# Two feed-forwards whose down products are formed by seven products a pair of chunks instead of eight

## The reference, cut to what matters

```python
# block 1, hidden width 2816 = 22 chunks of 128
g = h @ w_gate ; u = h @ w_up
x = x + (silu(g) * u) @ w_down
# block 2, hidden width 4096 = 32 chunks of 128
y = square(relu(h @ w_up_2)) @ w_down_2
x = x + rms_norm(y) * gain
```

## Time and profile before

| | us |
|---|---|
| median of 3 runs (758.26 to 759.86) | 758.54 |
| the profiled execution, its own time | 758.59 |
| its span, first to last instruction | 757.3 |
| TensorE busy | 739.8 |
| VectorE busy | 457.8 |
| ScalarE busy | 373.3 |
| GpSimd busy | 112.5 |
| transfers | 130.46 MB, mean 172 GB/s |

### The profile page before, as it was taken

The page is one execution under the profiler, slowest core; times in us unless marked ns, Lnnn a source line. Parts: engine busy times, 40 slices in busy tenths (PEclk is TensorE's granted clock), DMA queues, the critical chain, the costliest instruction groups (busy, mean ns, idle before and its releaser), DMA issues.

```text
span 757.3 us, 11043 instructions
## 1 busy us (share of the span) xinstructions
PE 739.8 (98%) x4394; PEld 641.1 (85%) x4394; DVE 457.8 (60%) x635; ACT 373.3 (49%) x535; POOL 112.5 (15%) x138
## 2 busy tenths in 40 slices
PE   6999999999999999999999999999999999999996
PEld 5877778999999999888888888888779899998895
DVE  5898695766555555465747555674948754455433
ACT  6666754644444434285443534664338644444431
POOL 2867550100000000001110000000302111001110
PEclk9999999999999999999999999999999999999999
DMA  9642142787665666446536543474535766656511
GB/s 318 207 132 82 58 160 92 229 284 220 189 212 172 195 216 208 133 142 219 169 110 195 194 139 112 123 250 147 178 107 198 260 192 187 206 184 191 180 46 56
DMA packets 70179, 130.46 MB, mean 172 GB/s; under 512 B 5312, under 2 KB 29072, under 8 KB 70128
## 3 DMA queue, kind: packets, MB, share of 16 engines
q1 hardware_dynamic: 68144, 125.00, 52.3%
q0 software_dynamic: 1552, 4.20, 1.7%
q10 hardware_dynamic: 432, 0.56, 0.2%
HBM read 128.62 MB, written 1.05 MB: 171 GB/s over the span
## 4 chain that ended last, share of the span: by engine, by line
PE 93%; DVE 3%; DMA 2%; issue 1%; ACT 1%; SPq 0%; DVEq 0%; ACTq 0%
PE psum L453 41%; PE psum L888 29%; PE psum L506 12%; PE psum L930 2%; DMA w_raw<-in_w_in 2%; PE psum L680 1%; PE psum L601 1%; PE psum L546 1%; PE psum L631 1%; PE psum L1058 1%; PE psum L582 1%; PE psum L652 1%; DVE b_ratio L2154 0%; PE psum L992 0%; PE psum L1020 0%
## 5 line engine op out<-in xcount | busy, mean ns | idle before, releaser
L1908 DVE TENSOR_TENSOR w_lo<-w_raw,w_hi 128x1024 fp32r<-128x1024 f32 x225 | 275.2, 1235 | 158.3 <-ACT w_hi L1284 157.7
L1284 ACT ACTIVATE w_hi<-w_raw 128x1024 fp32r<-128x1024 f32 x231 | 241.2, 1059 | 180.7 <-PE psum L888 78.6
L888 PE MATMUL psum<-h_hi,w_hi 128*128 128x256 f32 x608 | 170.3, 284 | 0.6 <-issue 0.6
L888 PE MATMUL psum<-h_hi,w_lo 128*128 128x256 f32 x608 | 169.5, 283 | 0.0
L888 PE MATMUL psum<-h_lo,w_hi 128*128 128x256 f32 x608 | 161.8, 281 | 0.0
L888 PEld LDWEIGHTS psum<-h_hi,w_hi 128*128 128x128 f32 x608 | 114.7, 189 | 1.7 <-issue 0.7
L888 PEld LDWEIGHTS psum<-h_hi,w_lo 128*128 128x128 f32 x608 | 114.4, 188 | 0.0
L888 PEld LDWEIGHTS psum<-h_lo,w_hi 128*128 128x128 f32 x608 | 111.1, 189 | 0.7
L453 PE MATMUL psum<-w_hi,h_hi 128*128 128x512 f32 (+1 forms) x240 | 94.5, 394 | 0.0
L453 PE MATMUL psum<-w_hi,h_lo 128*128 128x512 f32 (+1 forms) x240 | 93.0, 387 | 0.0
L453 PE MATMUL psum<-w_lo,h_hi 128*128 128x512 f32 (+1 forms) x240 | 92.9, 387 | 0.0
(11 more groups left out here) (303 smaller groups left out, 992.7 us busy)
## 6 DMA issues: line engine op xcount, KB each, us to landing
w_raw<-in_w_in SPq DMA_DIRECT2D x77, 512.0 KB, 4.5
w_raw<-in_w_down SPq DMA_DIRECT2D x54, 512.0 KB, 4.3
w_raw<-in_w_up SPq DMA_DIRECT2D x32, 512.0 KB, 4.4
w_raw<-in_w_gate SPq DMA_DIRECT2D x44, 256.0 KB, 2.9
w_raw<-in_w_up SPq DMA_DIRECT2D x44, 256.0 KB, 3.4
w_raw<-in_w_out SPq DMA_DIRECT2D x16, 512.0 KB, 4.0
w_raw<-in_w_branch_a SPq DMA_DIRECT2D x4, 512.0 KB, 4.6
w_raw<-in_w_branch_b SPq DMA_DIRECT2D x4, 512.0 KB, 4.6
```

The costliest lines, as they stand in the source:

```text
L888: mm = pe.matmul(outs, x[:, cols], y[:, kc, :], start=kc == 0 and n == 0, stop=kc == KC - 1 and n == (1 if i == 0 else 2))
L1284: act.activation(T.w_hi[:, k % SLOTS, :], T.w_raw[:, k % RAW_SLOTS, :], ACT.Copy).then_inc(S.w_rounded, 1)
L1908: dve.tensor_tensor(T.w_lo[:, k % SLOTS, :], T.w_raw[:, k % RAW_SLOTS, :], T.w_hi[:, k % SLOTS, :], ALU.subtract).then_inc(S.w_cut, 1)
```

## The change

The hidden width is taken in pairs of chunks. For one pair the down product is a product of a 2 by 2 block matrix (two token tiles by two chunks) with a 2 by 2 block matrix (two chunks by two halves of the width): eight products of blocks. The changed kernel forms them by seven products (the Strassen-Winograd form). The sums of blocks that the seven products need are formed per pair: four sums of hidden blocks on VectorE (`sum_hidden`, `sum_hidden_2`, `sum_hidden_3`; blocks of 128x128), and four sums of weight blocks (128x512). Two of these sums are made by a transfer that adds into its destination, issued by GpSimd (`add_pair`), onto two copies of one block that SyncE loads with a broadcast source (`load_pair`); the other two are made by VectorE (`sum_pair`, `sum_pair_rest`). All seven weight blocks and seven hidden blocks are then rounded and cut. The seven products of all pairs add up in seven PSUM banks, and the four results are formed from the banks once at the end of each block (`form`, `form_last`). The last pair of each feed-forward is done plainly in eight products (`down_quarters`).

Seven banks for products leave one bank for the up product, so ScalarE copies the up product out of it at once (`take_up`, `take_hidden`). The up weights are laid out so that a fill is one chunk of 128 columns over the whole depth of 1024 (block 1: one fill of gate and one of up a chunk), and they are taken out of the ring of eight slots: four slots for up fills, four reused by one of the two pair buffers. GpSimd no longer squares in block 2.

```diff
+def quarters(w):
+    v = w.reshape(w.shape[0] // (2 * P), 2, P, 2, WIDE)
+    order = ((0, 0), (1, 1), (1, 0), (0, 1))
+    return np.ascontiguousarray(np.stack([v[:, c, :, n, :] for c, n in order], axis=2))
...
+        for f in range(2 * PAIRS1):
+            self.first["up1", f] = len(self.fills)
+            for w in range(2):
+                self.fills.append([(lambda raw: raw, a["up1"][f, :, w, :])])
...
+        for f in range(2 * PAIRS2):
+            self.first["up2", f] = len(self.fills)
+            self.fills.append([(lambda raw: raw, a["up2"][f])])
+        self.pairs = [a["down1"][i] for i in range(PAIRS1)] + [a["down2"][i] for i in range(PAIRS2)]
...
+PRODUCT = {1: (1, 0, 2), 2: (3, 2, 0), 3: (7, 1, 1), 4: (2, 6, 6), 5: (5, 3, 5), 6: (6, 5, 3), 7: (4, 4, 4)}
+EARLY, LATE, LAST = (1, 2, 3), (7, 5, 6, 4), (1, 6, 7, 4, 5, 2, 3)
+NEEDS = {1: 1, 2: 1, 3: 1, 7: 2, 5: 2, 6: 3, 4: 3}
+QUARTER_BANKS = {1: ((0, 0, 7), (1, 0, 2), (0, 1, 3), (1, 1, 4)), 2: ((0, 0, 7), (0, 1, 2), (1, 0, 3), (1, 1, 4))}
...
+    def load_pair(q):
+        raw = pair_place(q)[1]
+        if q == 0:
+            sp.wait_ge(S.cut_done, CUT["h2"] + 4)
+        elif q == 1:
+            sp.wait_ge(S.x_squared, 4)
+        elif q == FIRST2:
+            sp.wait_ge(S.attended2, TILES * HEADS2)
+            sp.wait_ge(S.x_added, 12)
+        elif q == FIRST2 + 1:
+            sp.wait_ge(S.x_squared, 8)
+        else:
+            sp.wait_ge(S.pair_cut, pair_parts(q - 1))
+        n = 1 if q in (LAST1, LAST2) else 2
+        sp.dma_start(T.pair_t[:, raw, 0:n, :], W.pairs[q][:, 3:4, :].broadcast_to([P, n, WIDE])).then_inc(S.pair_landed[raw], 16)
+        sp.dma_start(T.pair_raw[raw], W.pairs[q][:, 0:3, :]).then_inc(S.pair_landed[raw], 16)
...
+        j1, j2 = k - W.first["up1", 0], k - W.first["up2", 0]
+        if j1 % 4 == 3 and 4 < j1 < 4 * PAIRS1:
+            load_pair((j1 - 7) // 4)
+        if j1 == 4 * PAIRS1 - 1:
+            load_pair(LAST1)
+        if j2 % 2 == 1 and j2 > 2:
+            load_pair(FIRST2 + (j2 - 3) // 2)
+    load_pair(LAST2)
...
+    def up_first(name, ready, rounded, spread, right=None):
+        k0 = W.first[name, 0]
+        for s, two in ((0, 0), (1, 0), (0, 1), (1, 1), (2, 0), (2, 1), (3, 0), (3, 1)):
+            ks = (k0 + 2 * two, k0 + 2 * two + 1)
+            if s == 0:
+                for k in ks:
                     pe.wait_ge(*W.cut(S, k))
-                    if c % 2 == 0:
-                        pe.wait_ge(S.hidden_cut, cut0 + (steps - 1) * cut_per + c // 2 + 1)
-                s = k % SLOTS
-                for n, (x, y) in enumerate(((T.hid_hi, T.w_hi), (T.hid_hi, T.w_lo), (T.hid_lo, T.w_hi))):
-                    mm = pe.matmul(bank[4 + 2 * t + h][:], x[last][:, c, t * P:(t + 1) * P], y[:, s, cols],
-                                   start=False, stop=c == chunks - 1 and n == 2)
-                if n_bank == 3:
-                    mm.then_inc(S.w_used, 1)
-            if n_bank < 3:
-                mm.then_inc(S.bank_done, 1)
-    feed_forward("up1", "down1", FFN1_STEPS, 2, CUT["h2"], lambda i: (S.hidden_done, i + 1), 0, 1, True, NORM["h2"],
-                 turn_x_right)
-    turn_pairs(T.x, (0, 1), (2, 3), [[(S.x_added, 9), (S.hidden_done, 11)], [(S.x_added, 10)]])
-    turn_pairs(T.x, (2, 3), (4, 6), [[(S.x_added, 11)], [(S.x_added, 12)]])
+            if spread and (s, two) == (3, 0):
+                spread_scale()
+            for c in range(2):
+                pe.wait_ge(*((S.norm_rounded, rounded + s + 1) if c == 0 else (S.cut_rounded, ready + s + 1)))
+                for k in ks:
+                    up_chunk(k, 2 * s + c, bank[4 + k - k0][:, 0:SEQ], (0, 2), 1)
+            pe.wait_ge(S.cut_done, ready + s + 1)
+            for c in range(2):
+                for k in ks:
+                    mm = up_chunk(k, 2 * s + c, bank[4 + k - k0][:, 0:SEQ], (1,), 1)
+                    if 2 * s + c == KC - 1:
+                        mm.then_inc(S.w_used, 1)
+            if (s, two) == (0, 0) and right is not None:
+                right()
...
+    def down(q, products, first=False, last=False):
+        buf, i = pair_place(q)
+        pe.wait_ge(S.hidden_cut, q + 1)
+        for n_product, p in enumerate(products):
+            x, y, b = PRODUCT[p]
+            pe.wait_ge(S.pair_cut, pair_parts(q) + NEEDS[p])
+            x_hi, x_lo = T.hid_hi[:, i, x - 1, :], T.hid_lo[:, i, x - 1, :]
+            y_hi, y_lo = T.pair_hi[buf][:, y, :], T.pair_lo[buf][:, y, :]
+            for n, (u, v) in enumerate(((x_hi, y_hi), (x_hi, y_lo), (x_lo, y_hi))):
+                mm = pe.matmul(bank[b][:], u, v, start=first and n == 0, stop=last and n == 2)
+            if last:
+                mm.then_inc(S.product_done, 1)
+        if products == LATE:
+            mm.then_inc(S.pair_used, 1)
+    def down_quarters(block):
+        q = (LAST1, LAST2)[block - 1]
+        buf, i = pair_place(q)
+        pe.wait_ge(S.hidden_cut, q + 1)
+        pe.wait_ge(S.pair_cut, pair_parts(q) + 2)
+        for t, half, b in QUARTER_BANKS[block]:
+            if b != 7:
+                pe.wait_ge(S.formed, 3 * (block - 1) + max(1, b - 2))
+            for c in range(2):
+                y = ((0, 3), (2, 1))[c][half]
+                x_hi, x_lo = T.hid_hi[:, i, 2 * c + t, :], T.hid_lo[:, i, 2 * c + t, :]
+                y_hi, y_lo = T.pair_hi[buf][:, y, :], T.pair_lo[buf][:, y, :]
+                for n, (u, v) in enumerate(((x_hi, y_hi), (x_hi, y_lo), (x_lo, y_hi))):
+                    mm = pe.matmul(bank[b][:], u, v, start=c == 0 and n == 0, stop=c == 1 and n == 2)
+            mm.then_inc(S.quarter_done, 1)
...
+    up_first("up1", CUT["h2"], NORM["h2"], True, turn_x_right)
+    up_two(W.first["up1", 2], 3)
+    pe.wait_ge(S.up_taken, 2)
+    up_two(W.first["up1", 3], 7)
+    for i in range(2, PAIRS1):
+        if i == 2:
+            pe.wait_ge(S.spread_copied, 1)
+        down(i - 2, EARLY, first=i == 2)
+        chunk_up1(2 * i)
+        if i == 2:
+            pe.wait_ge(S.up_taken, 3)
+        down(i - 2, LATE, first=i == 2)
+        chunk_up1(2 * i + 1)
+    down(LAST1 - 1, LAST, last=True)
+    pe.wait_ge(S.up_taken, 2 * PAIRS1)
+    down_quarters(1)
...
+    up_first("up2", CUT["h4"], NORM["h4"], False)
+    up_two(W.first["up2", 4], 3)
+    for i in range(2, PAIRS2):
+        if i > 2:
+            pe.wait_ge(S.up_taken, 2 * PAIRS1 + i)
+            up_two(W.first["up2", 2 * i], 7)
+        else:
+            pe.wait_ge(S.up_taken, 2 * PAIRS1 + 2)
+        down(FIRST2 + i - 2, EARLY, first=i == 2)
+        if i == 2:
+            pe.wait_ge(S.up_taken, 2 * PAIRS1 + 3)
+        down(FIRST2 + i - 2, LATE, first=i == 2)
+    down(LAST2 - 1, LAST, last=True)
+    pe.wait_ge(S.up_taken, 2 * PAIRS1 + PAIRS2)
+    down_quarters(2)
...
+    take_up(0)
+    take_up(1)
+    round_fill(f + 6)
+    silu(0)
+    round_fill(f + 7)
+    silu(1)
+    for i in range(1, PAIRS1):
+        round_pair(i - 1, 0)
+        take_up(2 * i)
+        round_fill(f + 4 * i + 4)
+        silu(2 * i)
+        round_fill(f + 4 * i + 5)
+        round_hidden(i - 1)
+        round_pair(i - 1, 1)
+        round_pair(i - 1, 2)
+        if i == LAST1:
+            round_quarters(LAST1, 0)
+            round_quarters(LAST1, 1)
+        take_up(2 * i + 1)
+        round_fill(f + 4 * i + 6)
+        silu(2 * i + 1)
+        round_fill(f + 4 * i + 7)
+    round_hidden(LAST1)
+    copy_first(1)
...
+    round_to(f + 8)
+    round_pair(FIRST2, 0)
+    take_hidden(0)
+    take_hidden(1)
+    square_hidden(0)
+    square_hidden(1)
+    for i in range(2, PAIRS2 + 1):
+        q = FIRST2 + i - 1
+        if i == 2:
+            round_pair(FIRST2, 1)
+            round_pair(FIRST2, 2)
+            round_hidden(FIRST2)
+        if i < PAIRS2:
+            for part in range(3):
+                round_pair(q, part)
+            take_hidden(i)
+            round_to(min(f + 2 * i + 6, len(W.fills)))
+            square_hidden(i)
+        else:
+            for part in range(2):
+                round_quarters(q, part)
+        round_hidden(q)
+    copy_first(2)
...
+    def sum_pair(q):
+        i = pair_place(q)[1]
+        dve.wait_ge(S.pair_cut, pair_parts(q) + 1)
+        dve.wait_ge(S.pair_added[i], pair_adds(q))
+        step(dve.tensor_tensor(T.pair_raw[i][:, 0, :], T.pair_t[:, i, 0, :], T.pair_raw[i][:, 1, :], ALU.add))
+    def sum_pair_rest(q):
+        i = pair_place(q)[1]
+        own()
+        dve.tensor_tensor(T.pair_raw[i][:, 2, :], T.pair_raw[i][:, 0, :], T.pair_raw[i][:, 2, :],
+                          ALU.add).then_inc(S.pair_summed, 1)
...
+    for i in range(1, PAIRS1):
+        sum_hidden(i - 1, 2 * i)
+        cut_pair(i - 1, 0)
+        sum_hidden_2(i - 1)
+        scale_gate(2 * i)
+        sum_hidden_3(i - 1)
+        cut_fill(f + 4 * i + 4)
+        sum_pair(i - 1)
+        times_up(2 * i)
+        sum_pair_rest(i - 1)
+        cut_fill(f + 4 * i + 5)
+        cut_hidden(i - 1)
+        cut_pair(i - 1, 1)
+        cut_pair(i - 1, 2)
```

(111 more changed lines are left out.)

448 lines of the change are left out of this document (247 added, 201 removed).

## The result

The changed kernel takes 783.5 us (median of 4 runs, 780.5 to 793.7), the kernel before 758.7 beside it: ratio 1.031, 95% interval 1.028 to 1.034. The run of 793.7 was in a slower state of the chip, and the ratio leaves it out; the other three have a median of 783.4. The forecast was 760.2, its range 751.5 to 771. It is 24.8 us slower, where 1.6 was forecast.

What follows compares the result with a forecast made beforehand. TensorE, busy 739.8 of 757.3 us, was taken as the bound. Of 17.5 us of matmuls saved, seams gave all back: block 1 gains 2.4, block 2 loses 4.0, span 758.9, time 760.2, range 751.5 to 771.

Steps and rivals of the forecast that it cites:

- The failed step: Block 2's rounds: the adding transfer, at most 3 us, begins as the fills end and is hidden.
- the 9.6 us: Block 2's rounds: loop of pair load, fills, cut and rounding takes 9.6 us, under the round of 10.6.
- 9.5 of 10.6: Block 2's rounds: with adds at half rate (2.9 us), transfers take 9.5 of 10.6 us, same result with less room.
- seam 4: Start of block 2's feed-forward: fill 7 lands late, at 583.8, first hidden cut ends 592.9; TensorE loses 5.2 us.
- Seam 5: Block 2's first pair: TensorE waits 3.3 us for ScalarE to empty bank 3; the pair ends at 601.1.
- tail behind it: End of block 2: VectorE's forming, scaling and additions after the last matmul grow from 3.2 to 8.7 us.
- about 17: Whole kernel: sign that TensorE's busy time falls by about 17 us.
- Seam 1: Start of block 1's feed-forward: the first down matmul starts at 156.0, as before (155.90).
- Step 3: End of block 1: from 303.8, last hidden cut after 6.2 us, block 2 starts 16.5 later, at 320.3.
- B: Rival: transfers bound block 2 if the add takes over 4 us of engine time; 763 to 773, middle 768; chance 0.19.
- C: Rival: the ScalarE and VectorE loop bounds block 2, 11.0 us instead of 9.85 without overlap; 765 us; chance 0.14.
- A: Rival: the seams are cheap, as their chains lie beside TensorE's work; 753.7 us; chance 0.27.

Runs made afterwards that it cites:

- experiment 5: Changed kernel with block 2's 15 adding transfers turned into plain copies to an idle buffer that nothing waits for; 770.6 us (ratio 1.014).
- experiment 1: Changed kernel with block 2's 15 adding transfers sent into an idle buffer, so nothing waits for them; 777.5 us (ratio 1.026).
- 3: Changed kernel with block 2's pair loads issued behind the next two up fills instead of ahead, adds kept; 784.5 us (ratio 1.034).
- Experiment 6: Changed kernel without block 2's adding transfers and with its pair loads issued behind the next two up fills; 765.7 us (ratio 1.008).
- 2: Changed kernel with block 2's adding transfers left out altogether; 767.7 us (ratio 1.012).

## Why the prediction was wrong

**The failed step** is the sentence on the adding transfer: "It then begins as the fills end, and hides." Its price was right. Over the whole changed kernel the queue's time is 0.117 x 782.1 - 0.017 x 757.3 = 78.6 us for 25 adds, 3.1 each, where "at most 3" was taken. The Trainium skill, "Collectives: The Full Stack", section "The bandwidth ceiling: the fold count and why AG ≠ RS ≠ AR", says of the add in a collective's ReduceScatter that it needs two source reads and so has half the rate of a copy; for this transfer experiment 5 agrees, 2.9 us against 1.6. Two things made of that price were wrong.

First, the add is a link of the pair's own loop, in series, and I had left it out of the 9.6 us (whose own terms, 7.8 + 9 - 7.0, make 9.8). Load 9.7, add 8.8, sums and cuts 4.5 and hand-offs make 23.7 us for two rounds. With the median landing of 5.5 for the add the same loop would take 20.4, an estimate, and fit into two rounds of 10.6. So it is not the add as such that breaks the loop, but the adds that go out beside the next pair's load: they begin as the fills end, as forecast, and don't hide. TensorE's two long waits and the one of 1.7 us ahead of 679.24 each follow on such an add, landed at 617.6, 744.2 and 675.8.

Second, I compared engine time with the round (9.5 of 10.6) and took room for 1.1 us. At that share a transfer doesn't land after its engine time: the fills on the chain of experiment 1 land after 10 to 13 us, the adds on the chains of 3 and of the changed kernel after 8.8 to 12.6, where the kernel before has 4.4 and 5.9. A window of block 2 in the changed kernel (columns as in rows 6):
```profile
592.00:746.00 154.00, 140.38 (x878) 125.20 (x877) 125.36 (x146) 94.45 (x104) 11.06 (x13) 0.98 0.79 234
```
0.79 of a round of 11.8 is 9.3 us: about the engine time of the forecast, in a longer round. The engines are not full on average, but work comes in bursts (pair load, two fills, add) whose parts wait for each other.

**The terms one by one.** Experiment 6 is the changed kernel without the adds of block 2, and its order, worth some 2 us, differs too. From seam 4 on the prediction counts in times of the kernel before, in which block 2 starts at 322.7. Its own block 2 starts 2.4 earlier, at 320.3, and its Sum takes that off; so the last matmul that it put at 750.0 stands here at 747.6, and the last addition, 758.7, at 756.3:

| | forecast | changed | without adds (6) |
|---|---|---|---|
| rounds, block 1 | 16.4 | 16.25 | as changed |
| block 2 starts | 320.3 | 324.9 | 323.9 |
| first pair's products end, from block 2's start | 278.4 | 281.7 | 282.4 |
| rounds, block 2 | 10.6 | 11.8 | 10.5 |
| last matmul ends | 747.6 | 770.9 | 754.1 |
| tail behind it | 8.7 | 8.6 | 8.5 |
| last addition ends | 756.3 | 779.5 | 762.6 |

The two rows of the changed kernel that end it, last matmul and last additions:
```profile
770.53 0.40 PE L1050 MATMUL psum<-w_hi,hidden_lo 128*128 128x512 f32 x1
...
778.11 1.41 DVE x L2894 x2
```
So the 23.2 us between forecast and result are 16.9 of block 2's adds (779.5 - 762.6) and 6.3 that experiment 6 has too: 3.6 of block 2's late start and 2.7 within it. What is dearer there is seam 4: from block 2's start the first down matmul comes after 274.0 us in experiment 6 and 273.5 in the changed kernel, forecast 270.2. Its fill 7 takes 10.0 us to land, at 264.1 and 263.6 from block 2's start, forecast 261.1. The rounds of 6 give 1.3 back. Seam 5 is right (8.2 us in the changed kernel, 8.4 in 6, forecast 8.2), the tail to 0.2 us, and the rounds of 6 show the matmuls of a round saved. TensorE's busy time fell by 5.7 us only, and by 11.1 in experiment 6, where the prediction's sign was "about 17": part of the matmuls ran at the lower clock, which the sum put at nothing. The granted clock of the changed kernel is 0.61 from 575 to 583 and 0.57 from 598 to 602, each behind a wait of 3.0 us. That the kernel would be no faster was forecast from the seams, and experiment 6, 6 us slower than before without any add in block 2, bears that out.

**Block 1.** Seam 1 put the first down matmul at 156.0. It comes at 157.5, the first nine take 3.7 us instead of 2.1 (granted clock 0.57 from 157.5 to 161.2), and the shorter rounds give half of that back: the last pair's products start at 305.4, forecast 303.8. Step 3 let VectorE cut "1.7 + 0.6" of the last pair's weights at 303.8 and come to the hidden cut 6.2 later. In the changed kernel the hidden cut ends at 312.7 instead of 310.0, since 4.5 us of cuts stand from 304.56 on, and the first two of them, the pair before's, I had not counted there. The timeline of VectorE:
```profile
312.03 0.68 DVE L2654 TENSOR_TENSOR hidden_lo<-hidden,hidden_hi 128x512 fp32r<-128x512 f32 x1
```
From there to block 2's start it is 12.2 us instead of 10.3, with GpSimd's two halves of an addition on the chain. 2.7 and 1.9 make the 4.6.

**The rivals.** B named the right effect, and its sign showed (pair blocks and up fills waited for, though not in each round), but its threshold was wrong: it wanted more than 4 us of engine time, and 3.1 sufficed. It gave 773 at most; the end of the range was drawn from that. The upper bound of the add (5.9, a round of 12.5, 784 us) gave nearly the measured time, but that is luck: the adds' engine time was 3.1 us and not 5.9, the rounds were 11.8 and not 12.5, and the seams brought the rest. Leaving it out was the choice that cost the range: 5.9 was the only landing of a GpSimd transfer of that size that the rows had, a plain one. C fails: without adds TensorE sets the rounds. A fails: no seam of the table came out cheaper than forecast by more than 0.2 us, and block 1's end and seam 4 were dearer.

What stays open: experiments 1 and 2 split the adds' cost in 6.0 of waiting and 9.8 of traffic in this order only; taken away in the other order the shares could differ, since each limit hides the other. That an add is slow because the next pair's load goes out beside it is read from when the thirteen were issued; no run moved the one against the other and held the rest. Block 2's late start of 3.6 us is one draw of a start that scatters from 322.1 to 327.5.
